# A hybrid decoder step on one core: a load sent behind four moves on SyncE's queue, and four weight loads that leave ScalarE's queue later

## The chip, the core and the metric

The kernel runs on one core of a Trainium2 chip. The time is that of the device in microseconds. Three runs took 1929.67, 1930.08 and 1934.85 us; the median is 1930.08. The profiled execution is the one of 1934.85 us, and its span, from the first to the last instruction, is 1933.1 us.

The engines are named as in the profile: PE (TensorE, the matmuls; PEld its weight loads), DVE (VectorE), ACT (ScalarE), POOL (GpSimd) and SP (SyncE, which issues most DMAs here). Each has its own program and runs it in order; semaphores tie them together. An instruction that waits holds up everything behind it on its engine.

## The reference

One step of a decoder with two layers, for 256 tokens of a new sequence and 8 sequences of 8 new tokens each (320 tokens, width 2048). The first layer is RWKV-7 time mixing: projections r, k, v, g, two small ones for decay and a, and then a recurrence over tokens for each of 32 heads of 64 channels. The second layer is stick-breaking attention over a shared K and V. Only the first one's recurrence matters here:

```python
def step(S, inp):
    r_t, w_t, k_t, v_t, kk_t, a_t = inp
    sa = jnp.einsum("bhvk,bhk->bhv", S, -kk_t)
    S = (S * w_t[:, :, None, :] + sa[..., None] * (kk_t * a_t)[:, :, None, :]
         + v_t[..., None] * k_t[:, :, None, :])
    o_t = jnp.einsum("bhvk,bhk->bhv", S, r_t)
    return S, o_t
```

Before it, `k` is multiplied by `1 + (a - 1) * k_a`, and `kk` is the normalised `k * k_k`. After it the output is normalised per head, a bonus `(r * k * r_k) v` is added, and the result is gated and projected by `w_o`.

## The kernel before

The kernel has three stages: the opening with the projections of layer one (to about 497 us), the recurrence (to about 827 us), and the trunk (the output projection, shared K/V, attention). The function `recurrence` does the second stage in 16 tiles of 128 channels (two heads). The tokens are cut into chunks of 64, so that the recurrence becomes small matmuls on 64 x 64 blocks.

A tile passes three parts: F (front: gates, normalisation, decay), P (products inside the chunks) and R (the run over the chunks). The work goes in **slots**: in slot s the engines do F of tile s, P of tile s - 1 and R of tile s - 2. In which order the steps stand in an engine's program is told by one list, `ORDER`, with names such as `F.a.ka1` (part F, engine a = ACT, step ka1; t is PE, v is DVE, g is POOL). `AT[name]` is a step's place in that list, from 0 to 1 of a slot. Every stream of steps is a Python generator that yields the place of its next step, and `side_by_side` always takes the one whose place is the smallest. So the number in a `yield` decides where the code behind it stands in its engine's program, and nothing else.

The steps that the prediction speaks of:

- `F.a.ka1` (L1293, on ACT): `k2 = a * k_a + (1 - k_a)`. It reads the tile `rw_in_a`. POOL's `k2`, `ID` and `csm` come behind it, and on ACT the copies of U and X, and all else of the slot.
- `F.g.ka` (L1214, on POOL): `ka = kk * a`, the last reader of `rw_in_a`. There is one buffer for it, so the next tile's `a` may be loaded only behind this step.
- `P.a.Bn` (L1307, on ACT): copies the transposed B. Behind it SP moves four blocks of it between partitions (`move_blocks`, L1087, four DMAs of 20 KB).
- `loads_a` (on SP): waits for `ka`, loads `a` of the next tile (L1074, 160 KB). Its place is just ahead of `P.a.Bn`. The loads of v and g, of the same size, follow the moves.
- `load_weights` (on ACT, L1377): in slots 4, 6, 8 and 10 it sends one DMA of 1 MB with a quarter of the weights for the output projection, which is needed only after 750 us. Its place is just behind `F.a.ka1`, in ACT's own DMA queue. SP's DMAs have another queue; all go over the same 16 DMA engines.

The last entries of `ORDER` are `P.v.Vn` and `R.v.ST3`; the last steps of ACT in a slot are the copies of O2 and O3 (L1337), and a new slot begins on ACT with `sq` and `kk0` (L1281, L1277).

Of the kernel before, what the change touches and what calls it, by code (L numbers as in the profile page):

```python
# [21 lines left out]
P = 128  # L22
# [133 lines left out]
def act_split(c_, act, g_all, q):  # L156

    act.wait_ge(c_.w_in[q], 16 * g_all + 16)

    if isinstance(g_all, int) and g_all == 0 and q < 2:  # L160
        pass
    elif q == 0:
        act.wait_ge(c_.chunk_used, 3 * g_all)
    elif q == 1:
        act.wait_ge(c_.bank_full, 4 * g_all)
    else:
        act.wait_ge(c_.chunk_used, 3 * g_all + q - 1)
    act.activation(c_.whi[:, q % 2], c_.wraw[:, q], ACT.Copy).then_inc(c_.whi_ready, 1)  # L168
# [201 lines left out]
AT = {x: k / len(ORDER) for k, x in enumerate(ORDER)}  # L370
# [33 lines left out]
def split_piece(c_, act, g_all, q, k):  # L404

    if k == 0:
        act.wait_ge(c_.w_in[q], 16 * g_all + 16)
        if q < 2:
            act.wait_ge(c_.bank_full, 4 * g_all)
        else:  # L410
            act.wait_ge(c_.chunk_used, 3 * g_all + q - 1)
    piece = act.activation(c_.whi[:, q % 2, k], c_.wraw[:, q, k], ACT.Copy)
    if k == QC - 1:
        piece.then_inc(c_.whi_ready, 1)
# [582 lines left out]
def recurrence(nc, c_, a):  # L997

    with ExitStack() as ctx:
# [6 lines left out]
        F, Q, R = (Stage(nc, ctx, x) for x in "FPR")  # L1006
# [62 lines left out]
        def _(sp):  # L1069
# [3 lines left out]
            def load(x, t):  # L1073
                sp.dma_start(ins[x][:], spilled(x, t)).then_inc(s_in[x], 16)  # L1074
# [38 lines left out]
                load("r", t + 1)  # L1113

            def loads_a(t):
                yield min(AT["F.g.ka"], AT["P.a.Bn"] - 0.0005)
                F.g.wait(sp, "ka", t)
                load("a", t + 1)

# [46 lines left out]
            for slot in range(TILES + 3):  # L1166
                if slot == 2:
                    store_gate(3)
                elif slot == 3:
                    sp.wait_ge(c_.stored, g_stored)  # L1170
                none = iter(())
                t, p, u = slot, slot - 1, slot - 2
                g = u - behind("R.g.y")
                ahead = t + 1 < TILES
                side_by_side(states(p) if 0 <= p < TILES else none,
                             loads_s(t) if ahead else none, loads_k(t) if ahead else none,
                             loads_r(t) if ahead else none, loads_a(t) if ahead else none,
                             loads_v(t) if ahead else none,
                             loads_blocks_of_v(p) if 0 <= p < TILES - 1 else none,
                             moves(p) if 0 <= p < TILES else none,  # L1180
                             stores_wkvp(u) if 0 <= u < TILES else none, stores_wkv(u) if 0 <= u < TILES else none,
                             loads_g(g) if 0 <= g < TILES - 1 else none)
# [70 lines left out]
        def _(act):  # L1253
# [110 lines left out]
            def gate(grp, m):  # L1364
                n, ps = 4 * (grp - 3) + m + 2, gate_banks[m] if grp == 3 else psP[:, m, 0:TOK]
                act.wait_ge(c_.bank_full, 4 * (FIRST_WO - 4 + grp) + m + 1)
                if grp == 3 and m == 0:
                    act.wait_ge(c_.stored, g_stored - 16)
                act.activation(stage[:, m], ps, ACT.Exp, scale=-1.0).then_inc(gate_done, 1)
                act.wait_ge(gate_done, 2 * n - 1)  # L1370
                act.activation(stage[:, m], stage[:, m], ACT.Ln, bias=c_.ones[:, 0:1]).then_inc(gate_done, 1)
                act.wait_ge(gate_done, 2 * n)
                act.activation(stage[:, m], stage[:, m], ACT.Exp, scale=-1.0).then_inc(c_.sig_ready, 1)

            def load_weights(i):
                act.wait_ge(c_.wlo_ready, 4 * FIRST_WO)
                act.dma_start(c_.wraw[:, i], weight_chunk(c_, PB["wo"], 0, i)).then_inc(c_.w_in[i], 16)  # L1377

            def beside(slot):
                if slot == 0:  # L1380
                    yield -0.02
                    gate(2, 3)
                    for q in range(1, 4):
                        yield 0.36 * (q - 1) + 0.02
                        act_split(c_, act, LAST_G, q)
                    yield 0.985
                    gate(3, 0)
                elif slot == 1:
                    for m, after in ((1, 0.65), (2, 0.9), (3, 0.97)):
                        yield after  # L1390
                        gate(3, m)
                elif slot in (4, 6, 8, 10):
                    yield AT["F.a.ka1"] + 0.0005
                    load_weights(slot // 2 - 2)
                elif slot == TILES - 1:
                    for q in range(2):
                        for k in range(QC):
                            yield (QC * q + k) / 8 + 0.03
                            split_piece(c_, act, FIRST_WO, q, k)
                elif slot in (TILES + 1, TILES + 2):  # L1400
                    for k in range(QC):
                        yield 1.0 if slot == TILES + 1 else AT["R.a.xh"] + 0.0005 * (k + 1)
                        split_piece(c_, act, FIRST_WO, slot - TILES + 1, k)

            stages(front, products, run, beside)

        @block.vector
# [1550 lines left out]
```

## Time and profile before

| | |
|---|---|
| runs | 1929.67, 1930.08, 1934.85 us |
| profiled execution | 1934.85 us, span 1933.1 us |
| PE | busy 1796.3 us (93%) |
| DVE | busy 1033.6 us (53%) |
| ACT | busy 825.0 us (43%) |
| POOL | busy 261.9 us (14%) |
| mean granted TensorE clock | 0.980 |
| the recurrence | from about 497 to 827 us |
| in it, a slot's length | about 15.5 to 19.6 us |

A line of the stretches gives the length of each stretch and how long each engine was busy in it, with the number of its instructions; "PEclk" is the granted clock as a share of the full 2.4 GHz. A line of the timeline has the start, the duration, the engine and the line of the source, the operation and the names of what it writes and reads; "[0.79 <-PE ...]" is the idle time of the engine ahead of it and what ended that. SPq and ACTq are DMAs being issued by SP and ACT: the duration is that of the issue alone. How long a DMA takes to land stands in the DMA view. "issue" as what ended a wait means that the profile shows nothing that the engine waited for.

### The profile page before, as it was taken

The numbers are of one execution on the slowest core, as the hardware profiler recorded it, in microseconds if no ns is written. First come the engines' busy times: TensorE is split into PE (matmuls) and PEld (weight loads), VectorE is DVE, ScalarE is ACT, GpSimd is POOL, SyncE is SP. The second block draws the span as 40 slices with busy tenths as digits, with TensorE's granted clock in tenths as the row PEclk, the third lists the DMA queues.
The fourth block names the chain that finished last, engine by engine and source line by source line (L and its number), as shares of the span: only waits on it lengthen the run. The fifth ranks groups of instructions, "written<-read, shape, count | busy, mean of one in ns | idle before, by whom it ended". The sixth has DMA issues, their size and how long they took to land.

```text
span 1933.1 us, 44071 instructions
## 1 busy us (share of the span) xinstructions
PE 1796.3 (93%) x18432; PEld 1525.4 (79%) x18432; DVE 1033.6 (53%) x1654; ACT 825.0 (43%) x1555; POOL 261.9 (14%) x331
## 2 busy tenths in 40 slices
PE   7999999999999999999999998999998998777897
PEld 6988999999878888799987676777776776444697
DVE  6744454453588888345445534343463444676334
ACT  4324233332577778433333332333334444555233
POOL 0300000000255566232000000000000001010032
PEclk9999999999999999999999999999999999899899
DMA  7534544554355544244889999999999999999541
GB/s 276 187 136 177 177 161 164 179 176 153 106 135 141 151 118 104 95 149 138 338 302 420 419 419 414 415 426 425 414 425 417 421 426 364 418 379 377 199 147 72
DMA packets 154202, 510.45 MB, mean 264 GB/s; under 512 B 60098, under 2 KB 81987, under 8 KB 108739
## 3 DMA queue, kind: packets, MB, share of 16 engines
q1 hardware_dynamic: 153442, 503.66, 69.0%
q10 hardware_dynamic: 576, 4.19, 0.6%
q8 instruction: 134, 2.20, 0.5%
q14 instruction: 50, 0.40, 0.1%
HBM read 472.86 MB, written 32.32 MB: 261 GB/s over the span
## 4 chain that ended last, share of the span: by engine, by line
PE 34%; DMA 17%; DVE 2%; issue 1%; ACT 1%; SPq 1%; DVEq 0%; ACTq 0%
DMA at_vraw<-in_cache_v 17%; PE psP L2669 8%; PE psP L2670 8%; PE psP L2671 8%; PE at_psO L2723 5%; PE at_psS L2702 3%; SPq L2082 1%; PE psP L2768 0%; PE at_psT L2714 0%; SPq L2122 0%; DVE at_w L2519 0%; PE psP L2790 0%; PE psP L2813 0%; DVE at_o_new L2586 0%; ACT at_p_w L2389 0%
## 5 line engine op out<-in xcount | busy, mean ns | idle before, releaser
L2669 PE MATMUL psP<-xhi,whi 128*128 128x320 f32 x1488 | 475.7, 320 | 2.9 <-DVE xlo L2556 1.9
L2671 PE MATMUL psP<-xhi,wlo 128*128 128x320 f32 x1488 | 460.7, 310 | 0.0
L2670 PE MATMUL psP<-xlo,whi 128*128 128x320 f32 x1488 | 460.6, 310 | 0.0
L2669 PEld LDWEIGHTS psP<-xhi,whi 128*128 128x128 f32 x1488 | 280.4, 188 | 65.8 <-issue 62.9
L2431 DVE TENSOR_TENSOR wlo<-wraw,whi 128x2048 fp32r<-128x2048 f32 x92 | 212.9, 2314 | 205.0 <-ACT whi L2257 204.7
L2257 ACT ACTIVATE whi<-wraw 128x2048 fp32r<-128x2048 f32 x92 | 176.0, 1913 | 276.0 <-PE psP L2671 274.7
L2670 PEld LDWEIGHTS psP<-xlo,whi 128*128 128x128 f32 x1488 | 280.8, 189 | 0.1
L2671 PEld LDWEIGHTS psP<-xhi,wlo 128*128 128x128 f32 x1488 | 280.4, 188 | 0.0
L139 PE MATMUL psP<-xhi,whi 128*128 128x320 f32 x704 | 218.1, 310 | 2.4 <-DVE wlo L174 2.3
L140 PE MATMUL psP<-xlo,whi 128*128 128x320 f32 x704 | 217.5, 309 | 0.0
L141 PE MATMUL psP<-xhi,wlo 128*128 128x320 f32 x704 | 217.5, 309 | 0.0
L174 DVE TENSOR_TENSOR wlo<-wraw,whi 128x2048 fp32r<-128x2048 f32 x47 | 108.4, 2306 | 138.9 <-ACT whi L168 138.9
L2723 PE MATMUL at_psO<-at_vraw,at_st 128*32 128x512 f32 x1000 | 129.4, 637 | 54.7 <-DMA at_vraw<-in_cache_v 47.4
L168 ACT ACTIVATE whi<-wraw 128x2048 fp32r<-128x2048 f32 x47 | 89.8, 1911 | 163.0 <-PE psP L141 161.6
L139 PEld LDWEIGHTS psP<-xhi,whi 128*128 128x128 f32 x704 | 132.2, 188 | 3.5 <-DVE wlo L174 2.9
L140 PEld LDWEIGHTS psP<-xlo,whi 128*128 128x128 f32 x704 | 132.2, 188 | 0.1
L141 PEld LDWEIGHTS psP<-xhi,wlo 128*128 128x128 f32 x704 | 132.2, 188 | 0.0
L2702 PE MATMUL at_psS<-at_kraw,at_qp 128*32 128x256 f32 x2048 | 125.8, 387 | 0.7 <-DMA at_kraw<-in_cache_k 0.7
L2723 PEld LDWEIGHTS at_psO<-at_vraw,at_st 128*32 128x32 f32 x1000 | 27.5, 112 | 108.7 <-DMA at_vraw<-in_cache_v 56.7
L2334 ACT ACTIVATE at_st<-at_psT 128x256 f32<-128x256 f32 x64 | 24.3, 380 | 204.4 <-PE at_psT L2714 204.4
L2702 PEld LDWEIGHTS at_psS<-at_kraw,at_qp 128*32 128x32 f32 x2048 | 60.9, 111 | 47.2 <-issue 13.5
L2516 DVE SCALAR_TENSOR_TENSOR at_w<-at_z,at_w 128x256 f32<-128x256 f32 x64 | 27.3, 427 | 122.5 <-ACT at_w L2323 122.5
(382 smaller groups left out, 3095.9 us busy)
## 6 DMA issues: line engine op xcount, KB each, us to landing
wraw<-in_weights SPq DMA_DIRECT2D x156, 1024.0 KB, 6.0
at_kraw<-in_cache_k SPq DMA_DIRECT2D x96, 1024.0 KB, 11.1
at_vraw<-in_cache_v SPq DMA_DIRECT2D x94, 1024.0 KB, 10.9
at_kraw<-in_cache_k SPq DMA_DIRECT2D x64, 512.0 KB, 9.9
at_vraw<-in_cache_v SPq DMA_DIRECT2D x62, 512.0 KB, 10.9
rw_s0t<-in_s0T SPq DMA_DIRECT2D x16, 256.0 KB, 3.4
o_wkv_s<-rw_SN SPq DMA_DIRECT2D x16, 256.0 KB, 2.7
wraw<-in_weights ACTq DMA_DIRECT2D x4, 1024.0 KB, 6.1
```

The source lines that it names most:

```text
L139: pe.matmul(out, wh, c_.xhi[:, kc, :], start=(kc == 0), stop=False)
L140: pe.matmul(out, wh, c_.xlo[:, kc, :], start=False, stop=False)
L141: last = pe.matmul(out, wl, c_.xhi[:, kc, :], start=False, stop=(kc == NM - 1))
L168: act.activation(c_.whi[:, q % 2], c_.wraw[:, q], ACT.Copy).then_inc(c_.whi_ready, 1)
L174: dve.tensor_tensor(c_.wlo[:, q % 2], c_.wraw[:, q], c_.whi[:, q % 2], ALU.subtract).then_inc(c_.wlo_ready, 1)
L2257: act.activation(whi[:, i % 2], wraw[:, q], ACT.Copy).then_inc(c_.whi_ready, 1)
L2431: dve.tensor_tensor(wlo[:, i % 2], wraw[:, q], whi[:, i % 2], ALU.subtract).then_inc(c_.wlo_ready, 1)
L2669: pe.matmul(out, wh, c_.xhi[:, kc, :], start=(kc == 0), stop=False)
L2670: pe.matmul(out, wh, c_.xlo[:, kc, :], start=False, stop=False)
L2671: last = pe.matmul(out, wl, c_.xhi[:, kc, :], start=False, stop=(kc == NM - 1))
L2702: last = pe.matmul(psS[32 * j:32 * j + 32, 0:BK].rearrange("p (t s) -> p t s", t=KB), qp[:, b % 2, j, 32 * i:32 * i + 32], keys, start=(i ...
L2723: last = pe.matmul(psO[32 * g:32 * g + 32, :], st[:, k % 2, pg, 32 * g:32 * g + 32], values_of(k, pg, g), start=(k % NBLK == 0 and pg == 0 ...
```

## The change

Two places in `recurrence` change, both the number in a `yield`.

```diff
             def loads_a(t):
-                yield min(AT["F.g.ka"], AT["P.a.Bn"] - 0.0005)
+                yield max(AT["F.a.ka1"], AT["F.g.ka"])
                 F.g.wait(sp, "ka", t)
                 load("a", t + 1)
```

```diff
                 elif slot in (4, 6, 8, 10):
-                    yield AT["F.a.ka1"] + 0.0005
+                    yield AT["P.v.Vn"]
                     load_weights(slot // 2 - 2)
```

No instruction is added or removed, and PE, DVE and POOL have the same programs as before. On SP, in the middle of a slot, `rw_in_a` is the load of `a` for the next tile, `rw_Bn` are the four moves, `rw_in_v` and `rw_VS` loads of v (this is slot 1; every later slot up to the one of the last tile changes alike).

```order
 L1087 DMA rw_Kn<-rw_KT 32x5x32 x4
 L1074 DMA rw_in_r<-spill_r 128x320
-L1074 DMA rw_in_a<-spill_a 128x320
-L1087 DMA rw_Bn<-rw_BT 32x5x32 x4
+L1087 DMA rw_Bn<-rw_BT 32x5x32 x4
+L1074 DMA rw_in_a<-spill_a 128x320
 L1074 DMA rw_in_v<-spill_v 128x320
 L1081 DMA rw_VS<-spill_v 32x10x32 x4
```

The load of `a` and its wait for POOL now stand behind the four moves and their wait for ACT, and directly ahead of v.

On ACT, before, at the start of slot 4: two copies of the slot before (L1337), `sq`, `kk0`, `Pc`, `Ht`, then `ka1` (L1293) and behind it the weight load.

```order
L1337 ACTIVATE stage_a<-rw_psR 128x64 x2
L1281 ACTIVATE rw_sq<-rw_in_k,vec 64x320 x2
L1277 ACTIVATE rw_kk<-rw_in_k,vec 128x320
L1265 ACTIVATE rw_PC<-rw_cs 128x320
L1312 ACTIVATE rw_Ht<-psP 128x4x32
L1293 ACTIVATE rw_k<-rw_in_a,rw_less_ka,vec 128x320
L1377 DMA wraw<-in_weights 128x2048
L1331 ACTIVATE rw_U<-rw_psR 128x64
```

On ACT now, from the end of slot 4 to the start of slot 5:

```order
L1331 ACTIVATE rw_SA<-rw_psR 128x64
L1337 ACTIVATE stage_a<-rw_psR 128x64 x2
L1377 DMA wraw<-in_weights 128x2048
L1281 ACTIVATE rw_sq<-rw_in_k,vec 64x320 x2
L1277 ACTIVATE rw_kk<-rw_in_k,vec 128x320
L1265 ACTIVATE rw_PC<-rw_cs 128x320
L1312 ACTIVATE rw_Ht<-psP 128x4x32
L1293 ACTIVATE rw_k<-rw_in_a,rw_less_ka,vec 128x320
L1331 ACTIVATE rw_U<-rw_psR 128x64
```

The weight load has moved past the whole rest of its slot and stands between the last copy of the slot and `sq` of the next, ahead of that slot's `ka1`. The same holds for the other three, so the loads leave at the start of slots 5, 7, 9 and 11 instead of 4, 6, 8 and 10.

## Rows read from the trace of the kernel before

**Rows 1.** Stretches of one slot each: start:end length, busy us, PEclk, DMA share, GB/s.
```profile
570.20:586.84 16.64, 15.31 (x431) 13.46 (x429) 14.12 (x32) 13.30 (x44) 10.46 (x13) 1.00 0.62 173
586.84:602.47 15.63, 15.25 (x431) 13.24 (x429) 14.41 (x34) 13.10 (x44) 10.33 (x14) 1.00 0.54 125
602.47:622.05 19.58, 16.75 (x431) 14.81 (x429) 14.37 (x32) 13.36 (x44) 10.19 (x13) 0.91 0.53 153
...
637.68:655.93 18.25, 15.31 (x431) 13.26 (x429) 13.77 (x32) 13.20 (x44) 9.96 (x14) 1.00 0.58 167
...
672.20:690.91 18.71, 16.70 (x431) 13.98 (x428) 13.51 (x33) 13.35 (x44) 10.25 (x14) 0.91 0.61 163
...
722.58:738.03 15.45, 15.07 (x431) 13.17 (x429) 14.10 (x32) 13.14 (x44) 10.50 (x13) 1.00 0.47 123
```

**Rows 2.** Waits of PE, 540 to 760: us in total, times, longest.
```profile
PE rw_psR L1699 <- issue: 4.5, 2, 2.6
PE psP L1626 <- issue: 3.2, 3, 2.4
...
PE rw_psR L1731 <- issue: 0.9, 1, 0.9
```

**Rows 3.** Timeline of PE, slot 6: start, us, instruction, idle before.
```profile
607.05 0.27 PE L1626 MATMUL psP<-rw_W,rw_D2t 64*64 64x64 f32 x2 [2.44 <-issue]
```

**Rows 4.** DMA queues, 597.0 to 604.6: packets, MB, share of 16 engines (q8 has none).
```profile
q10 hardware_dynamic: 125, 1.00, 38.5%
```

**Rows 5.** DMA queues, 604.6 to 605.2.
```profile
q8 instruction: 1, 0.02, 10.0%
```

**Rows 6.** A stretch behind the stall of slot 6; PEclk is third from last.
```profile
607.80:611.20 3.40, 3.40 (x72) 3.40 (x70) 2.06 (x6) 2.21 (x8) 2.25 (x3) 0.50 0.25 63
```

**Rows 7.** Timeline of SP: DMAs issued, slots 4 to 7.
```profile
583.75 0.59 SPq L1074 DMA_DIRECT2D rw_in_v<-spill_v  x1
...
595.03 0.33 SPq L1074 DMA_DIRECT2D rw_in_a<-spill_a  x1
595.40 3.12 SPq L1087 DMA_DIRECT2D rw_Bn<-rw_BT  x4
598.56 0.59 SPq L1074 DMA_DIRECT2D rw_in_v<-spill_v  x1
599.20 0.43 SPq L1074 DMA_DIRECT2D rw_in_g<-spill_g  x1
...
634.48 0.59 SPq L1074 DMA_DIRECT2D rw_in_v<-spill_v  x1
```

**Rows 8.** Timeline of ACT, slots 5 to 8.
```profile
584.48 0.64 ACT L1293 ACTIVATE rw_k<-rw_in_a,rw_less_ka,vec 128x320 f32<-128x320 f32 x1
...
594.00 0.46 ACT L1307 ACTIVATE rw_Bn<-rw_BT 128x320 f32<-128x320 f32 x1
...
597.72 0.22 ACT L1337 ACTIVATE stage_a<-rw_psR 128x64 f32<-128x64 f32 x1 [0.79 <-PE rw_psR L1699]
...
599.55 0.33 ACTq L1377 DMA_DIRECT2D wraw<-in_weights  x1
...
600.11 0.64 ACT L1293 ACTIVATE rw_k<-rw_in_a,rw_less_ka,vec 128x320 f32<-128x320 f32 x1
600.66 0.21 ACT L1331 ACTIVATE rw_U<-rw_psR 128x64 f32<-128x64 f32 x1
...
634.76 0.33 ACTq L1377 DMA_DIRECT2D wraw<-in_weights  x1
```

**Rows 9.** Landing of v and g (sent 598.56, 599.20), then v (634.48): KB, us.
```profile
rw_in_v<-spill_v SPq DMA_DIRECT2D x1, 160.0 KB, 2.6
rw_in_g<-spill_g SPq DMA_DIRECT2D x1, 160.0 KB, 5.7
...
rw_in_v<-spill_v SPq DMA_DIRECT2D x1, 160.0 KB, 4.8
```

**Rows 10.** All DMAs of the tile `rw_in_g`: us from issue to landing.
```profile
DMA to landing us min/median/max: 2.3/3.2/7.3
```

## The prediction

> **What bounds the kernel now.** I first read the stretches that each hold one slot of the recurrence (from one `F.g.csm` on POOL to the next) [rows 1]. A slot without a weight load lasts 15.63 us (first of six) to 15.45 (last); the six, all between 586.8 and 738, average 15.78. The four stretches behind a weight load last 16.64, 19.58, 18.25 and 18.71: 73.18 in sum, against 4 x 15.78 = 63.12, so **the loads cost 10.1 us now**. In a quiet slot PE is busy for 15.3 us of 15.6, ACT for 13.1: whatever holds PE up lengthens the slot, and ACT has little to catch up with.
>
> Next, what PE waited for: 4.5 + 3.2 + 0.9 = 8.6 us went to "issue", in six idle pieces [rows 2]; these are almost all of PE's long gaps in this stage. The timeline has one of them: PE idle for 2.44 us before 607.05, on no semaphore [rows 3]. The DMA view says why. From 597.0 to 604.6, while the 1 MB weight load (q10) took 38.5% of the sixteen engines, not one packet of queue 8, kind "instruction", was served [rows 4]; one of 16 KB comes at 604.7 [rows 5], and PE goes on 2.3 us later. So the load costs what it does because PE's own instructions come late. Behind two of the four stalls the granted clock was 0.50 for 3.4 us [rows 6], the lower of the two levels (1.2 GHz); it lies in the slot of 19.58, which is 1.36 us longer than its stall explains (19.58 - 15.78 - 2.44); 3.4 us at half speed can cost 1.7 at most. I take 1.2 for such a fall; the slot of 18.71 has the other (PEclk 0.91 in both) [rows 1].
>
> **The change, part one: the order on SP.** Before, SP waits for `ka` of POOL, sends `rw_in_a` (the load of `a` for the next tile) at 595.03, then the four moves of Bn from 595.40, then v at 598.56 [rows 7]. Bn was ready at 594.46 [rows 8]. After it, the moves go at about 594.5, 0.94 us earlier, and `a` goes behind them: 4 moves took 3.12 us, so at 597.65 instead of 595.03, **2.6 us later**, in what was v's place less 0.9. Bn earlier buys nothing: none of PE's waits in rows 2 is for it. Who waits for `a` is ACT's `ka1` (L1293), at 600.11, 2.25 us after the slot's first ACT work could be sent (taken as 597.85, just behind the copy of 597.72) [rows 8]. Behind `ka1` in ACT's order stand the copy of U (600.66), on which PE's next product waits, and the rest of the slot; POOL's k2, ID and csm wait too. A load of this size in v's place, v itself, landed 2.6 us after its issue at 598.56 [rows 7, 9]. Quiet slots: 597.65 + 2.6 = 600.25, 0.1 late. One slot earlier v went at 583.75, and `ka1` ran at 584.48: 583.75 - 0.94 + 2.6 = 585.4, 0.9 late [rows 7, 8]. Over the 13 slots I expect 0 to 0.9 late and take 0.35 as the mean. It is lost whole, since ACT has no slack before its last copy, and in ten slots: **+3.5 us** (ends: 0, if ACT's 0.79 us of waiting before 597.72 takes it up, and 9).
>
> **Part two: the weight load.** It leaves its place behind `ka1` (599.55) and goes behind the last copy of the same slot, so to the start of the next one: about 597.85 on the clock of rows 8, in slots 5, 7, 9, 11 instead of 4, 6, 8, 10. Against the slot's start it moves by only 1.7 us, but it moves in front of `ka1`, and `a` is now under way: 597.65 against 597.85. What a load of 160 KB costs when it is sent about when the weights are, rows show twice. g, 0.35 us ahead of the weights (599.20, 599.55), landed 5.7 us after its issue; v, 0.28 ahead (634.48, 634.76), 4.8 after, where 2.6 is usual [rows 7 to 9]. g's longest is 7.3 [rows 10]. So `a` lands 4.5 to 7 us behind the weights' issue; I take 5.7, near g. `ka1` wants it at 2.25: **3.5 us late** (2.2 to 4.7). PE has 0.6 us of cover there, but ACT's 3.5 us remain, with PE, POOL and DVE behind it.
>
> Is `a` always caught? It escapes when sent 1 us or more ahead of the weights, as v was at 598.56 (0.99 ahead, landed in 2.6) [rows 7 to 9]. The two slots of rows 7 put `a` 0.2 us ahead of the weights and behind them; the moves of a slot vary by more than that, so I let one of four escape. In those PE's instruction fetch can be late too, but PE is idle anyway: the longer wait counts, not both. Half of such stalls are followed by the lower clock, 1.2 us each [rows 1, 6]. Sum: 3 x (3.5 + 0.6) + 1.0 for the fourth, where the fetch alone is late = **+13.3**. What goes away is **-10.1**. The other transfers of the slot start (g, VS, s, k, the state) meet the load as they do now, with half a slot to spare.
>
> The Trainium skill (DMA: Bandwidth & Descriptors, "Queues, rings and completion order") says that each DMA engine takes turns between the queues at packet granularity. By it `a`, on SP's queue, would share the engines and not wait for ACT's whole megabyte, and would land perhaps 1 us later than usual; that is rival B. The 5.7 and 4.8 us of rows 9 speak against so mild a price.
>
> The Trainium skill (Runtime: NRT & Kernel Launch, "Instruction fetch mechanics") has a sequencer fetch blocks of 16 KiB ahead through its own DMA queue, mostly hidden. The size agrees with rows 5; that it is hidden does not hold beside these loads. Were it hidden, the place of the load would be free, and the change would only lose part one.
>
> **Sum.** -10.1 + 13.3 + 3.5 = +6.7 us. The profiled execution took 1934.85 us (span 1933.1), so 1941.6 under the same conditions; it is 4.8 above the median of the runs, 1930.08. On the median: **1936.8 us**.
>
> **The rivals.**
> A, the forecast: `a` is caught by the load in about three slots, ACT waits for it. +6.7, with its own range of +3 to +12 (1933 to 1942).
> B, `a` is not caught: it shares the engines with the weights, or goes out a microsecond earlier because SP no longer waits for POOL. Then only PE's fetch is late. The load begins 1.7 us earlier in the slot, and PE's fetches of 16 KB fall where its program puts them, elsewhere in the odd slots than in the even; half of the stalls vanish or shrink: some 3 us stay of 10.1, plus 2 of lateness: -5, **1925 us**. For it: the place moved against a fixed rhythm of fetches, and v at 598.56 was not caught. Against it: rows 9.
> C, the costs cancel: small lateness is taken up by ACT's wait at the slot's end, and the caught loads cost about what the fetches did. -10.1 + 10 + 1 = +1, **1931 us**. For it: both stalls come from one transfer, so their lengths are related. Against: `ka1` is hit at the start of its need, a fetch has some cover.
> D, the worse side: in all four slots `a` and the last Bn moves land with the weights, 4.7 us late, and each stall is long enough to bring the lower clock: 4 x (4.7 + 1.2) = 23.6, less 10.1, plus 3.5 = +17, **1947 us**. It decides from the point where all four `a` leave behind the weights. Against: SP's order lets `a` out before the slot starts in at least some slots.
> That the change doesn't do what it says is excluded for the order; it could do nothing for the time only as C.
>
> **How the numbers follow.** A 0.55, B 0.15, C 0.20, D 0.10. A measurement of this kernel tells 0.3% (5.8 us) from no change. Above 1935.9 lie all of D and two thirds of A (0.37): slower 0.47. Faster (under 1924.3): most of B and a little of C, 0.14. The rest, 0.39, is no change. The range, 1927 to 1945, holds A and C whole and leaves out most of B and D.
>
> **What would show it.** In the changed kernel: (1) `rw_in_a` stands behind four Bn moves on SP, sent within 0.5 us of the weights in slots 5, 7, 9, 11, and takes 5 to 7 us to land there against 2.6 elsewhere; (2) ACT idle before L1293 for some 3.5 us in three or four slots, released by the DMA of `rw_in_a`, and for a few tenths in many others; (3) "issue" waits of PE down from 8.6 us to under 4; (4) slots behind a load of 18.5 to 20 us, quiet ones of about 16.1 instead of 15.78; (5) nothing changed after 830 us. I am wrong if `a` lands within 3.5 us in the load slots (then B), or if quiet slots stay at 15.8 (then part one costs nothing and the sum is +3), or if stalls of "issue" stay at the new place, beside the wait for `a`.

## The result, and the profile after

The changed kernel is slower. In the first comparison its median was 1947.69 us (1944.29 to 1948.99, four runs; the profiled one comes on top) against 1929.88 us: **ratio 1.0087, interval 1.0062 to 1.0111**. It was timed twice more, each time beside the kernel before on one chip: 1.0050 (1.0027 to 1.0074) and 1.0059 (1.0039 to 1.0078). The first +17 us is the highest of the three; the later ones are +10 and +11, and all three intervals lie above 1. The forecast was +6.7 us, with the right sign and a mechanism that is there, but too small for the first comparison, whose median lies outside the range (1945). The medians of the other two (1940.19 and 1941.11) lie inside it.

The profiled execution took 1941.17 us (span 1939.4), 6.5 below the median of its timed runs, while that of before stood 5 above its own. So the two traces show less of a difference (+6.3) than the medians do. That the forecast for the profiled execution (1941.6) is met to 0.4 us is luck: that execution was the fastest of its five, and the terms below were off in opposite directions.

Waits of PE, 540 to 760, in the trace of the changed kernel: us in total, times, longest. It answers to [rows 2].

```profile
PE rw_psR L1699 <- ACT rw_X L1312: 10.5, 8, 3.6
...
PE rw_psR L1699 <- issue: 0.9, 1, 0.9
```

The waits for instructions are down from 8.6 to 0.9 us. In their place PE waits 10.5 us for the copy of X on ACT, the second instruction behind `ka1`. The same view of ACT says what ACT waited for:

```profile
ACT rw_k L1293 <- DMA rw_in_a<-spill_a: 13.6, 9, 3.9
```

13.6 us in nine slots, the longest 3.9; before the change no such wait was there. The timeline of ACT in slot 9, answering to [rows 8]:

```profile
648.04 0.22 ACT L1337 ACTIVATE stage_a<-rw_psR 128x64 f32<-128x64 f32 x1 [0.78 <-PE rw_psR L1699]
648.05 0.33 ACTq L1377 DMA_DIRECT2D wraw<-in_weights  x1
...
654.59 0.65 ACT L1293 ACTIVATE rw_k<-rw_in_a,rw_less_ka,vec 128x320 f32<-128x320 f32 x1 [3.93 <-DMA rw_in_a<-spill_a]
```

SP's queue in the same slot, answering to [rows 7], and then the landing of that one load:

```profile
645.17 4.25 SPq L1087 DMA_DIRECT2D rw_Bn<-rw_BT  x4
649.77 0.33 SPq L1074 DMA_DIRECT2D rw_in_a<-spill_a  x1
650.15 0.42 SPq L1074 DMA_DIRECT2D rw_in_v<-spill_v  x1
650.62 0.42 SPq L1074 DMA_DIRECT2D rw_in_g<-spill_g  x1
```

```profile
rw_in_a<-spill_a SPq DMA_DIRECT2D x1, 160.0 KB, 4.7
```

The weights left at 648.05, `a` at 649.77, and `a` landed 4.7 us later, 6.5 us after the weights' issue. In this slot `a` went out 1.7 us behind the weights, not the 0.2 ahead of the forecast. PE's product stood behind it:

```profile
655.66 0.48 PE L1699 MATMUL rw_psR<-rw_U,rw_X 64*64 64x64 f32 x4 [3.59 <-ACT rw_X L1312]
```

That is the forecast's picture. But it holds in two of the four load slots only. In slot 5 `a` left 0.68 us ahead of the weights and was in before `ka1` wanted it (timelines of SP and ACT, landing of that `a`):

```profile
580.71 0.59 SPq L1074 DMA_DIRECT2D rw_in_a<-spill_a  x1
581.39 0.39 ACTq L1377 DMA_DIRECT2D wraw<-in_weights  x1
583.96 0.64 ACT L1293 ACTIVATE rw_k<-rw_in_a,rw_less_ka,vec 128x320 f32<-128x320 f32 x1
```

```profile
rw_in_a<-spill_a SPq DMA_DIRECT2D x1, 160.0 KB, 2.7
```

What the forecast had not at all is in slot 4, where no weights move (timeline of ACT), and in the clock behind slot 9's stall (a stretch; the third number from the end is the granted clock's share):

```profile
567.10 0.65 ACT L1293 ACTIVATE rw_k<-rw_in_a,rw_less_ka,vec 128x320 f32<-128x320 f32 x1 [1.63 <-DMA rw_in_a<-spill_a]
```

```profile
655.40:662.00 6.60, 6.33 (x122) 6.31 (x124) 2.44 (x6) 4.43 (x15) 2.42 (x3) 0.50 0.42 111
```

ACT waited 1.63 us in a quiet slot, and behind the long stall the clock was at 0.50 (1.2 GHz) for all of these 6.6 us, where [rows 6] had 3.4. The slots, cut as in [rows 1]:

```profile
569.47:586.32 16.85, 16.28 (x423) 14.37 (x416) 13.98 (x32) 12.94 (x43) 10.31 (x13) 0.90 0.51 142
586.32:604.66 18.34, 15.72 (x433) 13.59 (x431) 14.43 (x33) 13.53 (x45) 10.19 (x14) 0.99 0.51 137
604.66:621.96 17.30, 16.30 (x437) 14.71 (x438) 14.42 (x32) 13.21 (x44) 10.33 (x14) 0.92 0.55 153
621.96:637.64 15.68, 15.22 (x433) 13.21 (x428) 14.24 (x32) 13.15 (x44) 10.33 (x13) 1.00 0.57 144
637.64:656.96 19.32, 15.21 (x413) 13.20 (x406) 14.38 (x33) 13.15 (x44) 10.32 (x14) 0.96 0.59 160
656.96:675.49 18.53, 17.72 (x449) 15.96 (x450) 14.62 (x32) 13.42 (x44) 10.21 (x13) 0.86 0.38 99
675.49:694.01 18.52, 15.21 (x415) 13.19 (x409) 14.31 (x32) 13.14 (x44) 10.31 (x13) 0.97 0.61 168
694.01:711.74 17.73, 17.41 (x438) 15.85 (x437) 13.60 (x32) 13.27 (x43) 10.24 (x13) 0.84 0.36 97
```

Stretches of 19.32 and 18.52 hold the stalls of slots 9 and 11; the two behind them, with no stall of that size, still take 18.53 and 17.73 at a clock of 0.86 and 0.84, with PE busy 17.7 and 17.4 us of them. So one caught `a` costs twice: 3.5 and 2.7 us in its own slot (19.32 and 18.52 less 15.78), and 2.75 and 1.95 us (18.53 and 17.73 less 15.78; part of the first is 0.85 us of ACT waiting for that slot's own `a`) while PE does the next slot's work slowly.

### The profile page after: what moved, and what is told of

Same layout as the page of the kernel before. It is cut to its first block, busy times and chain, and to the rows that moved or that the text cites. A ratio compares the mean times of both kernels' runs of the same rounds, so it can differ in the third digit from the quotient of the medians.

```text
span 1939.4 us, 44071 instructions
## 1 busy us (share of the span) xinstructions
PE 1799.4 (93%) x18432; PEld 1529.7 (79%) x18432; DVE 1035.4 (53%) x1654; ACT 825.2 (43%) x1555; POOL 262.2 (14%) x331
## 4 chain that ended last, share of the span: by engine, by line
PE 32%; DMA 18%; DVE 2%; issue 2%; ACT 1%; SPq 1%; DVEq 0%; ACTq 0%
DMA at_vraw<-in_cache_v 18%; PE psP L2669 8%; PE psP L2670 7%; PE psP L2671 7%; PE at_psO L2723 5%; PE at_psS L2702 3%; SPq L2082 1%; PE psP L2768 0%; PE at_psT L2714 0%; DVE at_o_new L2586 0%; SPq L2122 0%; ACT at_p_w L2389 0%; PE psP L2790 0%; ACT at_p_w L2387 0%; DVE at_w L2519 0%
```

## The experiments

All were timed in five rounds against the kernel before on the same chip, in three sessions (the first comparison is a fourth); us are the ratio's excess times 1930. The order on SP (old: `a`, Bn; new: Bn, `a`) and the place of the four weight loads make a table; each cell is a ratio with its interval.

| place of the loads | old order | new order |
|---|---|---|
| none (8 KB each) | 0.9946 (0.9929, 0.9963) | 0.9975 (0.9960, 0.9989) |
| behind `ka1`, slots 4, 6, 8, 10 | 1 (before) | 1.0019 (1.0000, 1.0037) |
| behind `ka1`, slots 5, 7, 9, 11 | 0.9995 (0.9976, 1.0013) | 1.0050 (1.0028, 1.0071) |
| end of slots 4, 6, 8, 10 | 0.9991 (0.9972, 1.0010) | 1.0087; 1.0050; 1.0059 (changed) |

**The order alone.**

```diff
-                yield min(AT["F.g.ka"], AT["P.a.Bn"] - 0.0005)
+                yield max(AT["F.a.ka1"], AT["F.g.ka"])
```

> Only the order on SP changes: the load of `a` stands behind the four Bn moves; the weight loads stay behind `ka1`. Theory T (late `a`): in every slot `a` lands a few tenths to 2 us after `ka1` could run, ACT waits for it in most slots, in sum 4 to 8 us, and the load slots stall for instructions as before: +4 to +8 us. Rival R (the collision alone): `a` is late only where the megabyte of weights is sent just ahead of it; here it never is, so within 2 us of the kernel before.

1.0019: +3.7 us, with an interval that just reaches no change, and a little under T's +4 to +8. ACT's waits in its trace:

```profile
ACT rw_k L1293 <- DMA rw_in_a<-spill_a: 7.5, 11, 1.7
```

Eleven waits where R allowed none. The time alone would not have told the two theories apart; this row does. PE stood on issue in two long pieces here too (3.2 and 2.0 us), as T had it.

**The place alone.**

```diff
-                    yield AT["F.a.ka1"] + 0.0005
+                    yield AT["P.v.Vn"]
```

> Only the weight loads move, to the end of slots 4, 6, 8, 10; the load of `a` stays ahead of the Bn moves, some 2.9 us before the weights. Theory T: `a` escapes and `ka1` does not wait; PE's late instructions shrink from 8.6 us to some 3: -5 us, at most 0. Rival R: the weights at the slot's start catch `a` or the last Bn moves anyway, and the product that reads Bn waits: +8 us or more.

0.9991, no change that can be measured. `a` escapes, but R was right about the moves, though not about their price (+8 us or more). Waits of PE in its trace, then the last of the four moves, sent 0.26 us ahead of the weights:

```profile
PE rw_psR L1699 <- DMA rw_Bn<-rw_BT: 5.7, 4, 2.0
```

```profile
rw_Bn<-rw_BT SPq DMA_DIRECT2D x1, 20.0 KB, 6.8
```

20 KB took 6.8 us. In all four load slots PE waited for this move, and never on issue. In the changed kernel, where the moves leave ahead of `a`, no wait of PE for them is in the trace. The loads cost 8.7 us here (0.9991 - 0.9946), 10.4 at their old place; the intervals do not tell the two apart, so the wait changed its name and, as far as can be measured, not its size. My expectation of fewer stalls on issue held, that of a gain did not: I had not counted the move as somebody's last input.

**No loads, old and new order.** Each load is cut to 8 KB; the rest of that data is left out.

```diff
-                act.dma_start(c_.wraw[:, i], weight_chunk(c_, PB["wo"], 0, i)).then_inc(c_.w_in[i], 16)
+                act.dma_start(c_.wraw[:, i, 0:1, 0:16], weight_chunk(c_, PB["wo"], 0, i)[:, 0:1, 0:16]).then_inc(c_.w_in[i], 16)
```

> The kernel before with the four weight loads cut to 8 KB each (all but 1/128 of that data is left out, so the output projection works on stale weights). It measures what the transfers cost at their old place. Theory T: the 8.6 us of PE's waits for instructions vanish and with them the lower clock: -10 us. Rival R: PE would be held by something else there, -3 us at most.

> The new order on SP with the four weight loads cut to 8 KB each (the same data is left out). Against the run without loads in the old order it measures the order alone, with no collision possible. Theory T: `a` is late by 0.35 to 0.7 us in ten slots or more, +4 to +8 us over that run, so -6 to -2 us against the kernel before. Rival R: the order costs nothing without the loads, both runs alike within 2 us.

Old order: 0.9946, **-10.4 us**; the forecast had 10.1 for what the loads cost at their old place. PE's waits on issue all but vanish with the load (waits of PE, old order without loads; the two issue rows of at least 0.2 us):

```profile
PE psP L1626 <- issue: 0.2, 1, 0.2
PE rw_psR L1699 <- issue: 0.2, 1, 0.2
```

New order: 0.9975, so **the order costs 0.29%, 5.6 us, with no megabyte in sight**. The forecast had 3.5, and from the two intervals the difference is known to some 4 us only, so 3.5 is not excluded. The two traces without loads differ by 8.8 us over thirteen slots (214.2 against 205.4 us from the `csm` of tile 2 to that of tile 15). In the new order's trace ACT waited ten times for `a`, the longest in slot 4:

```profile
ACT rw_k L1293 <- DMA rw_in_a<-spill_a: 8.1, 10, 1.7
```

```profile
565.68 0.59 SPq L1074 DMA_DIRECT2D rw_in_a<-spill_a  x1
566.31 0.43 SPq L1074 DMA_DIRECT2D rw_in_v<-spill_v  x1
566.79 0.43 SPq L1074 DMA_DIRECT2D rw_in_g<-spill_g  x1
```

```profile
rw_in_a<-spill_a SPq DMA_DIRECT2D x1, 160.0 KB, 4.1
```

```profile
571.30:578.10 6.80, 6.80 (x137) 6.74 (x135) 3.15 (x8) 4.19 (x15) 2.50 (x5) 0.50 0.45 111
```

These are, one after the other, the timeline of SP, the landing of that `a`, and a stretch behind it. `a` took 4.1 us, with v and g sent within 1.1 us behind it; PE stood for 1.3 us until 570.92, and then the clock was at 0.50 for 6.8 us. In old order without loads the clock fell once between 530 and 775, for 3.4 us; in new order it did so four times, for 17.1 us in all. In both, one fall of 3.4 us lies at the stage's start, behind a wait of 2.1 us that has nothing to do with `a`.

**The changed kernel again, twice.** No edit.

> The changed kernel once more, for its time on the same chip as the others and a second trace. Theory T (`a` is caught): +13 to +19 us, ACT waits for `a` 3 us or more in at least three of slots 5, 7, 9, 11. Rival (the first time was an outlier, the two parts add: +3.7 - 1.7): +2 us.

> The changed kernel a third time, for its size and a third trace. If the first time (+17) and the second (+10) are one distribution, the ratio lies between 1.004 and 1.010 here, and ACT waits for `a` 3 us or more in one to four of the load slots.

1.0050 and 1.0059; the third time lies where it was expected. The rival that the parts add (+3.7 - 1.7) is out; theory T's number of caught slots is not met in any trace. Slots 5, 7, 9, 11 had an ACT wait of 3 us or more in two (3.9, 3.1), one (4.25) and two (3.9, 3.7) of four.

Over the three traces that is five of twelve load slots, and in these traces the order of issue tells them apart. The seven `a` that went out 0.44 to 0.68 us ahead of the weights landed in 2.7 to 3.9 us, and ACT waited 0.8 us at most. The five that went out with the weights or up to 1.7 us behind them took 4.7 to 6.5 us. Each of these five was followed by 6.8 us at the lower clock. Their own slots were 3.5 us longer than 15.78 in the mean, and the slots behind them 2.3 (1.7 to 2.8).

ACT's waits in the two new traces:

```profile
ACT rw_k L1293 <- DMA rw_in_a<-spill_a: 8.6, 10, 4.2
```

```profile
ACT rw_k L1293 <- DMA rw_in_a<-spill_a: 13.5, 8, 3.9
```

The first of them was the fastest of its eight runs (1927.34; they reach to 1947.66). The kernel before has runs from 1923.16 to 1940.44 there. Which transfers meet differs from trace to trace, and a kernel's time is a mean over that.

**New order, loads behind `ka1` of the odd slots.**

```diff
-                elif slot in (4, 6, 8, 10):
-                    yield AT["P.v.Vn"]
-                    load_weights(slot // 2 - 2)
+                elif slot in (5, 7, 9, 11):
+                    yield AT["F.a.ka1"] + 0.0005
+                    load_weights((slot - 5) // 2)
```

> New order on SP, weight loads behind `ka1` in slots 5, 7, 9, 11: against the changed kernel they leave only 2 to 3 us later, but after `a` is in. Theory T: no `a` is caught, the cost is that of the order and of the loads at a harmless place, +2 to +6 us. Rival (the odd slots, or the order, are what costs): +12 us or more.

1.0050, +9.7 us: outside what either theory named, and as dear as the changed kernel. No long wait for `a` is in its trace (4.8 us in five, longest 1.7), but PE stood three times on issue:

```profile
PE rw_psR L1699 <- issue: 5.8, 2, 3.1
PE rw_psR L1699 <- ACT rw_X L1312: 3.3, 5, 1.3
PE rw_psR L1727 <- issue: 2.7, 1, 2.7
```

**The same in old order** (the kernel before, with the same slots and the load behind `ka1` as it was).

> The kernel before with the weight loads behind `ka1` of slots 5, 7, 9, 11 instead of 4, 6, 8, 10. It tells what the odd slots cost by themselves. Theory P (where a load stands against PE's fetches decides): three or four stalls on issue of about 2.7 us instead of 0.9 to 2.6, each with the lower clock behind it: +3 to +6 us. Rival (the slot's number is nothing; the new order on SP made the odd slots dear): within 2 us of the kernel before.

0.9995: no change that can be measured. In its trace PE waits on issue for 4.8 us in two pieces (longest 2.9) and 1.5 in one. Theory P, by which the odd slots are dear in themselves, falls. With the new order they cost 0.31% more than the even ones do, by intervals that still overlap; whether that is more than chance, and why, is left open.

**A quarter of each load** (the changed kernel; three quarters of that data are left out).

```diff
-                act.dma_start(c_.wraw[:, i], weight_chunk(c_, PB["wo"], 0, i)).then_inc(c_.w_in[i], 16)
+                act.dma_start(c_.wraw[:, i, 0:1], weight_chunk(c_, PB["wo"], 0, i)[:, 0:1]).then_inc(c_.w_in[i], 16)
```

> The changed kernel with each of the four weight loads cut to 256 KB (three quarters of that data are left out). Theory T: `a` is late by the time that the transfer holds the engines, so a quarter of the excess stays: the order's +5.7 less the loads' 10.4 gives -4.8, plus a quarter of 21.8: about 0 to +2 us. Rival (a fixed cost of two queues meeting, whatever the size): +10 us or more.

1.0018 (0.9999 to 1.0037), +3.5 us, a little above T's range, whose values the interval does not exclude, and far from the rival's. Over the new order without loads that is 8.3 us for a quarter of the bytes, where the whole loads cost 14.5 to 21.6. So the price grows with the size; a quarter of it would be 3.6 to 5.4 us, and the intervals do not tell whether it grows less than in proportion.

**Two buffers for `a`** (the changed kernel; the load waits for `ka` of the slot before and stands behind that of r, so ahead of the moves again). The second buffer and the lines that choose between the two are not shown.

```diff
-                yield max(AT["F.a.ka1"], AT["F.g.ka"])
-                F.g.wait(sp, "ka", t)
+                yield max(AT["F.g.Rz"], AT["F.v.rk"]) + 0.0002
+                F.a.wait(sp, "ka1", t)
+                if t:
+                    F.g.wait(sp, "ka", t - 1)
```

> The changed kernel with a second buffer for `a`: its load waits for `ka` of the slot before and goes right behind that of r, ahead of the Bn moves; the moves wait for ACT alone and the weights leave at the slot's end, as in the changed kernel. Theory T (ACT's wait for `a` is the whole loss): no wait of ACT for `a`, no lower clock in quiet slots; like the run with only the place changed or, as Bn leaves 0.5 us earlier, a little better: -2 to -6 us against the kernel before. Rival: the earlier moves of Bn or the weights' place cost by themselves: +5 us or more.

0.9988 (0.9970 to 1.0005), on the chip where the changed kernel had 1.0059: 0.7%, 13.7 us, are gone, as theory T had it. No wait for `a` is left in its trace; the last moves still meet the weights, as with the place alone:

```profile
PE rw_psR L1702 <- DMA rw_Bn<-rw_BT: 1.8, 3, 1.0
```

This is the strongest evidence that the late `a` is the changed kernel's whole loss. It gains nothing that can be measured over the place alone (0.9991), which sends `a` ahead of the moves without a second buffer, so SP's wait for POOL had cost nothing that can be measured either.

**The weights in pieces.** The old kernel, each load cut into four of 256 KB, sent in slots 4 to 11 behind `ka1` and behind `Pm`; nothing is left out of the computation. The function `load_piece` and a wait for the pieces at their reader are not shown.

```diff
-                elif slot in (4, 6, 8, 10):
-                    yield AT["F.a.ka1"] + 0.0005
-                    load_weights(slot // 2 - 2)
+                elif slot in range(4, 12):
+                    for k, place in enumerate(("F.a.ka1", "F.a.Pm")):
+                        yield AT[place] + 0.0005
+                        load_piece(slot // 2 - 2, 2 * (slot % 2) + k)
```

> The kernel before (old order), whole computation, with each weight load cut into four pieces of 256 KB, sent in slots 4 to 11, two a slot, behind `ka1` and behind `Pm`. Theory F (PE's instructions are held up as long as a transfer holds the engines): a piece of about 1.2 us is hidden by the instructions that PE still has: -6 to -10 us against the kernel before, no long wait on issue. Rival: eight more DMAs and twice as many slots touched cost as much as they save: within 3 us.

> The second buffer for `a` together with the weights in sixteen pieces, whole computation: the candidate for a kernel that beats both. Theory T: the pieces' gain (-7 us) and up to 2 us more from SP, which no longer waits for POOL ahead of Bn: -7 to -10 us. Rival: SP's wait costs nothing, so no more than the pieces alone, or less if a piece now meets a move: -4 to -7 us.

0.9964 (0.9947 to 0.9981), **-7 us**, as expected of theory F. Together with the second buffer: 0.9951 (0.9935 to 0.9967), -9.5 us, in T's range, median 1921.27 against 1929.81, nearly the 10.4 that the loads had cost. The two intervals overlap, so that the buffer adds something is not shown. Waits of PE on issue in the trace with the buffer:

```profile
PE psP L1633 <- issue: 1.0, 2, 0.6
```

1.0 us instead of 8.6, and no lower clock between 540 and 775. Both versions beat the kernel before and the changed one.

## Why the prediction was wrong

*The loads cost 10.1 us now, through PE's late instructions.* Right: 10.4 us went with them, and the stalls too. The traces bear the cause out further. At the four stalls of the kernel before PE has done 9234, 10770, 12562 and 14354 weight loads and matmuls. Each number is 18 more than a multiple of 256, and queue 8 brings its 16 KB about once in 254 of them.

*`a` moves 2.6 us later on SP, into v's old place; Bn earlier buys nothing.* Right for the order alone: without loads `a` went out 2.7 us ahead of ACT's `sq` in the mean in old order and 0.3 ahead in new order (slots 3 to 15). In the load slots of the changed kernel it went out from 0.68 us ahead of the weights to 1.7 behind them, where the forecast had 0.2 ahead. Bn earlier buys nothing with the loads at their old place. With the loads moved it does: 5.7 us of PE's waits for the last move, seen with the place alone, are not there in the changed kernel.

*The lower clock: half of the stalls in load slots, 1.2 us each, so 0.6 a slot, and nothing in quiet ones.* **This is the step that failed, in both terms of the sum.** All five caught slots of the three traces of the changed kernel had it behind them, for 6.8 us each, and the slot behind took 2.3 us more in the mean, not 0.6 (1.65 and 1.95 in the two where ACT had no wait of its own). My 1.2 us came from one fall of 3.4 us, and the half from two stalls in four. In quiet slots, PE's waits of 0.95 to 1.8 us for the copy of X had the lower clock behind them too, in these traces and in the one of the new order without loads.

*Quiet slots: 0.35 us late each, 3.5 us in sum.* The measured term is 5.6 us by the times, which do not exclude 3.5, and 8.8 by one pair of traces. In that pair, PE's idle pieces grew by 5.4 us; that leaves 3.4 for the 10.2 us at the lower clock which the new order has in those thirteen slots and the old one has not. ACT's lateness was 0.62 us a slot in the mean (8.1 in thirteen), and PE waited 5.5 us for the copy of X behind it, so it was not lost whole, as I had said. I took 2.6 us for `a` to land, from one v. In the new order it takes longer, even without the weights (DMAs of `rw_in_a`, 540 to 770, new order without loads; the same view of before has 2.2/2.6/3.4, of the changed kernel 2.4/3.3/5.0):

```profile
DMA to landing us min/median/max: 2.4/2.9/4.4
```

That v and g, sent within 1.1 us behind it, are the reason is an argument; no run separates it.

*Load slots: three of four caught, 3.5 us each and 0.6 for the clock, 13.3 in sum.* The mechanism is as forecast: where `a` went out with or behind the weights, it landed 5.7 to 6.8 us after their issue, ACT waited 3.1 to 4.25 us, and PE's stalls on issue shrank to one at most. The 3.5 us of a caught slot is right in the mean. Two things were off, in opposite directions. The hits were fewer, five of twelve instead of nine, because seven `a` went out 0.44 to 0.68 us ahead and escaped, where the forecast let them go free only from 1 us on. Each hit cost 5.8 us instead of 4.1, through the clock. By the times the term is 14.5, 16.2 or 21.6 us (changed kernel less new order without loads, in the three comparisons).

*The sum.* -10.1 + 13.3 + 3.5 became -10.4 + 5.6 + 14.5 to 21.6, so +10 to +17. Fewer hits made up in part for the dearer clock; so the forecast's nearness to the profiled execution comes of errors that cancel. Rival D named 17 us, but by all four slots being caught, which no trace shows. Rival B described seven of the twelve load slots, but not the other five, nor the cost of the order. Rival C (the costs cancel) fits the place alone and not the changed kernel.

*Turns between the queues.* The Trainium skill (DMA: Bandwidth & Descriptors, "Queues, rings and completion order") says that a DMA engine takes turns between the queues, packet by packet. My estimate from it, `a` about a microsecond later than usual, fits the seven `a` sent 0.44 to 0.68 us ahead of the weights (2.7 to 3.9 us). It does not fit the five sent later (4.7 to 6.5), nor a move of 20 KB that was sent 0.26 us ahead of a megabyte on the other queue and took 6.8 us; there the measurement decides against so mild a price. The rule itself is not contradicted, since no row shows the turns of one engine.

What stays open: why the odd slots seem dear only in the new order; and why the timed runs of the changed kernel lose more than its traces. From the `csm` of tile 2 to that of tile 15 two of the three traces take 8.4 and 9.6 us longer than the one of before (216.1) and one takes 0.7 less. So no trace shows the +17 us of the first comparison, and the step named above accounts for a part of the miss only.

## What to carry to other kernels

A single-buffered load whose reader comes early in the next round should leave as soon as its last reader is done. What stands ahead of it on its own queue makes it late in every round, and a large transfer sent with it or just ahead of it on another queue can hold it for several microseconds more. A large load for later use is better cut into pieces: in the one arrangement tried here, sixteen pieces of 256 KB at two places of the slot, most of its cost was gone. Where a chain of engines is nearly full, reckon behind a wait of TensorE of about a microsecond or more with some microseconds at the lower clock, and with its price in the next slot.

## What the runs showed of the hardware

A transfer of 1 MB on ACT's queue held up the fetch of PE's own instructions (queue 8, 16 KB each), and PE stood still for 0.9 to 3.2 us on no semaphore; with pieces of 256 KB the longest such wait was 1.0 us. Around a transfer of 1 MB on ACT's queue, 160 KB on SP's queue sent 0.44 to 0.68 us ahead of it landed in 2.7 to 3.9 us in the changed kernel's traces, and sent with it or behind it in 4.7 to 6.5. That is no sharp bound: in the kernel before one such load (g) sent 0.45 us ahead took 7.3 us, and in the changed one a move of 20 KB sent 1.3 us ahead took 6.6. The granted clock fell to 0.50 for 3.4 or 6.8 us behind waits of PE from 0.6 to 3.9 us, but not behind each: the stall of 2.63 us in slot 8 of the kernel before had none.
